# Three more projection chunks as seven products of quarter blocks, and the last block's sixteen selection rounds in one run

## The reference, cut to what matters

```
h = rmsnorm(x) ; z = h @ w_in          # 10 column groups
qa, ka, va (512 each), qi (4x64), ki (64), wi (4), qb, kb, vb, gb (512 each)
rope on qa, ka, qi, ki, qb, kb
indexer scores: sum over 4 heads of wi * relu(qi . ki), causal
per token: top 128 keys by that score (top 64 for a sample token)
a = softmax attention of 8 heads over the chosen keys only
b = retention of 8 heads with decay, group norm, gate
x = x + rmsnorm([a, b] @ w_out)
x = x + rmsnorm(relu(rmsnorm(x) @ w_up)^2 @ w_down)
```

## Time and profile before

| | us |
|---|---|
| median of 3 runs | 1571.54 (1571.03 to 1572.36) |
| the profiled execution's own time | 1573.14 |
| its span | 1571.4 |
| TensorE busy | 1547.7 (98%) |
| VectorE busy | 845.1 (54%) |
| ScalarE busy | 450.0 (29%) |
| GpSimd busy | 476.1 (30%) |

### The profile page before, as it was taken

How to read it: one execution, slowest core, us unless ns; L and a number is a source line. 1 busy time by engine, 2 the same in 40 slices (tenths; PEclk the granted TensorE clock), 3 DMA queues, 4 the chain that set the end, 5 groups by cost and what they waited for, 6 DMA issues and landing times.

```text
span 1571.4 us, 21618 instructions
## 1 busy us (share of the span) xinstructions
PE 1547.7 (98%) x7966; PEld 1154.9 (73%) x7966; DVE 845.1 (54%) x1708; ACT 450.0 (29%) x1045; POOL 476.1 (30%) x354
## 2 busy tenths in 40 slices
PE   8999999999999999999999999999999999999998
PEld 5445755688888888888844466556888888888887
DVE  4599679846652013333467977788366610132334
ACT  5222355225421003310242224551253200123101
POOL 0005201023653424345310051010146524234461
PEclk9999999999999999999999999999999999999999
DMA  6326311024332122222223272110243421322211
GB/s 211 131 72 215 135 55 54 3 86 133 131 112 88 74 108 81 86 73 84 94 72 108 81 235 89 54 55 14 74 147 122 135 80 54 112 103 81 80 55 55
DMA packets 52811, 150.40 MB, mean 96 GB/s; under 512 B 8250, under 2 KB 29506, under 8 KB 39394
## 3 DMA queue, kind: packets, MB, share of 16 engines
q1 hardware_dynamic: 45218, 140.65, 26.1%
q10 hardware_dynamic: 7488, 8.36, 1.5%
HBM read 139.79 MB, written 9.02 MB: 95 GB/s over the span
## 4 chain that ended last, share of the span: by engine, by line
PE 77%; DVE 18%; issue 2%; ACT 2%; POOL 0%; DMA 0%; ACTq 0%; DVEq 0%; POOLq 0%
PE ps L1186 46%; PE ps L806 9%; PE ps L1124 7%; PE ps L843 4%; DVE arena L1870 3%; DVE top L1868 3%; PE ps L771 1%; DVE x_feat L2024 1%; PE ps L784 1%; DVE arena L1814 1%; DVE arena L1816 1%; PE ps L971 1%; DVE rstd_ffn L1812 1%; PE ps L1082 1%; PE ps L994 1%
## 5 line engine op out<-in xcount | busy, mean ns | idle before, releaser
L806 PE MATMUL ps<-wring,h_feat 128*128 128x512 f32 (+1 forms) x704 | 316.3, 586 | 2.8 <-ACT h_feat L1309 2.5
L1186 PE MATMUL ps<-arena,wring 128*128 128x256 f32 (+1 forms) x1280 | 285.8, 382 | 0.3 <-DVE arena L2108 0.3
L1186 PEld LDWEIGHTS ps<-arena,wring 128*128 128x128 f32 x1280 | 243.0, 190 | 37.7 <-DVE arena L2108 1.1
L806 PEld LDWEIGHTS ps<-wring,h_feat 128*128 128x128 f32 x704 | 124.7, 190 | 125.7 <-issue 112.5
L2405 POOL TENSOR_TENSOR wring<-wring,arena 128x512 f32<-128x512 f32 (+1 forms) x48 | 78.8, 1641 | 345.3 <-PE ps L1186 321.9
L1186 PE MATMUL ps<-h_feat,wring 128*128 128x256 f32 (+1 forms) x768 | 176.6, 381 | 0.0
L1186 PEld LDWEIGHTS ps<-h_feat,wring 128*128 128x128 f32 x768 | 145.9, 190 | 21.6
L1186 PE MATMUL ps<-mix,wring 128*128 128x256 f32 (+1 forms) x512 | 120.2, 383 | 0.8 <-DVE p_sb L2082 0.8
L1186 PE MATMUL ps<-arena 128*128 128x264 f32 x512 | 119.1, 386 | 0.0
L1124 PE MATMUL ps<-mix,wring 128*128 128x256 f32 (+1 forms) x512 | 115.1, 384 | 0.8 <-ACT mix L1473 0.8
L2388 POOL TENSOR_TENSOR pt_sb<-pt_sb 128x256 f32<-128x256 f32 (+1 forms) x94 | 72.8, 774 | 126.4 <-ACT pt_sb L1283 123.1
(11 more groups left out here) (251 smaller groups left out, 2041.8 us busy)
## 6 DMA issues: line engine op xcount, KB each, us to landing
wring<-in_w_all SPq DMA_DIRECT2D x108, 1024.0 KB, 5.1
arena<-in_cache_k SPq DMA_DIRECT2D x32, 256.0 KB, 5.2
arena<-in_cache_v SPq DMA_DIRECT2D x32, 256.0 KB, 4.4
o_k_out<-arena ACTq DMA_DIRECT2D x2, 1024.0 KB
o_v_out<-arena ACTq DMA_DIRECT2D x2, 1024.0 KB
arena<-in_state SPq DMA_DIRECT2D x2, 1024.0 KB, 4.8
o_rets_out<-arena ACTq DMA_DIRECT2D x2, 1024.0 KB, 9.8
wring<-in_w_idx SPq DMA_DIRECT2D x3, 648.0 KB, 4.9
```

The lines of the kernel that those rows point to most:

```text
L806: last = mm(ps[:, bank_of(c, i), 0:width], h_feat[:, k, token_cols(t)], wt, start=(k == 0), stop=(k == KD - 1))
L1186: last = mm(out, a[:, j, :], b, start=(opens(n) and j == 0), stop=(j == nk - 1), skip_group_check=True)
```

## The change

`BLOCKED` becomes (1, 2, 3, 4, 5): chunks 1, 2 and 3 are done as seven products too. VectorE gets their five sums each, GpSimd their four weight sums each, ScalarE takes and scales quarters in place of whole tiles. The input's sums are made right at the layer's start; since in1's first place is needed for the indexer keys of the cache and the gate, it first lies in `mix`, and a fifth `input_sum` makes it again in its old place for chunk 5. The weight sums of chunk 1 lie in `qT`. The work beside the chunks gets new positions, the new keys of the samples (`new_key`) come after GpSimd's first sums of chunk 3, the value outputs are issued later, and `own_values(1)` one part earlier. The order on VectorE is written anew: block 1's rounds are spread over chunks 1 to 3, block 2's lie beside chunks 3 and 4, and block 3's sixteen rounds stand in one run after `chunk_c22(4)`, ahead of attention.

```diff
-BLOCKED = (4, 5)
+BLOCKED = (1, 2, 3, 4, 5)
...
+DOTS = [(3, 2), (4, 0), (4, 6), (5, 4), (6, 2), (7, 0)]
...
         def tokens_of(c):
-            return zr[1] if c == 4 else zr[0]
+            return {1: zr[1], 2: zr[0], 3: v_tok, 4: zr[1], 5: zr[0]}[c]
...
             def beside_q(i, k):
-                if (i, k) == (0, KD - 1):
+                if (i, k) == (2, 3):
...
                     pe.wait_ge(rope_done, past(rope_done) + TILES)
...
             def beside_qb(i, k):
...
-                if (i, k) in ((3, KD - 1), (6, 5)):
-                    g = (i - 3) // 3
+                if (i, k) in ((2, 3), (5, 3)):
+                    g = (i - 2) // 3
...
-                project(1, beside_q)
-                project(2, beside_k)
-                project(3, beside_v)
+                project_blocks(1, beside_q)
+                project_blocks(2, beside_k)
+                project_blocks(3, beside_v)
...
 VectorE, the layer's loop:
+                rope(1, NT)
+                for j in range(4):
+                    combine(j)
+                chunk_u2(1)
+                combine(4)
+                combine(5)
+                select_top(sc[1], top8[:], 1)
+                combine(6)
+                combine(7)
+                chunk_u3(1)
+                chunk_c22(1)
+                combine(8)
+                combine(9)
+                select_top(sc[1], top8[:], 1)
+                combine(10)
+                combine(11)
+                chunk_c12(1)
+                rope(1, 2)
+                rope(1, 3)
+                chunk_c21(1)
+                select_top(sc[1], top8[:], 1)
                 rope(1, 0)
...
+                rope(1, 1)
                 dve.wait_ge(ts_mm, past(ts_mm) + 1)
+                rope(2, NT)
...
+                select_top(works[:], tops[:], 4)
+                chunk_u2(2)
+                select_top(works[:], tops[:], TOPK_S // 8 - 4)
...
+                chunk_u3(2)
+                chunk_c22(2)
+                select_top(sc[1], top8[:], 2)
+                chunk_c12(2)
                 rope(2, 2)
                 rope(2, 3)
+                chunk_c21(2)
+                select_top(sc[1], top8[:], 1)
+                rope(2, 0)
+                rope(2, 1)
+                select_top(sc[1], top8[:], TOPK_P // 8 - 7)
+                block_mask(1)
+                chunk_u2(3)
+                select_top(sc[2], top8[:], 2)
+                chunk_u3(3)
+                chunk_c22(3)
...
-                select_top(sc[3], top8[:], 4)
+                chunk_c21(3)
+                select_top(sc[2], top8[:], 9)
                 chunk_u2(4)
-                select_top(sc[3], top8[:], TOPK_P // 8 - 15)
-                block_mask(3)
+                select_top(sc[2], top8[:], TOPK_P // 8 - 13)
+                block_mask(2)
                 own_values(0)
                 chunk_u3(4)
                 chunk_c22(4)
+                select_top(sc[3], top8[:], TOPK_P // 8)
+                block_mask(3)
...
 GpSimd, the layer's loop:
                 input_sum(1)
                 input_sum(2)
                 input_sum(3)
-                chunk_sum(4, 1)
-                chunk_sum(4, 2)
+                chunk_sum(1, 1)
+                chunk_sum(1, 2)
                 input_sum(4)
-                chunk_sum(4, 3)
-                chunk_sum(4, 4)
+                chunk_sum(1, 3)
+                chunk_sum(1, 4)
                 for n in range(1, 5):
-                    chunk_sum(5, n)
+                    chunk_sum(2, n)
+                chunk_sum(3, 1)
+                chunk_sum(3, 2)
+                for b in range(CSLOTS):
+                    new_key(b)
+                chunk_sum(3, 3)
+                for b in range(CSLOTS, NB):
+                    new_key(b)
+                chunk_sum(3, 4)
+                input_sum(5)
+                for c in (4, 5):
+                    for n in range(1, 5):
+                        chunk_sum(c, n)
```

More of the change, by code:

```diff
@@ L354, in quarter @@
             return a[:, at:at + 4 * 2 * P].rearrange("p (k n) -> p k n", n=2 * P)
-        in1, in2, in3, in4 = quarter(gate_flat, 3 * W), quarter(mix_high, 0), quarter(mix_high, 2 * W), quarter(temps, 0)
-        cs1, cs2 = quarter(kbd_flat, 0), quarter(kbd_flat, 2 * W)
+        in1, last_in1 = quarter(mix_flat, 0), quarter(gate_flat, 3 * W)
+        in2, in3, in4 = quarter(mix_high, 0), quarter(mix_high, 2 * W), quarter(temps, 0)
+        first_cs, cs = [[quarter(a, 2 * i * W) for i in range(2)] for a in (qT.rearrange("p h n -> p (h n)"), kbd_flat)]
         raw = [temps[:, i * W:(i + 1) * W] for i in range(3)]
@@ L578, in tokens_of, with sums_of_chunk, first_sum_of @@
         def tokens_of(c):
-            return zr[1] if c == 4 else zr[0]
+            return {1: zr[1], 2: zr[0], 3: v_tok, 4: zr[1], 5: zr[0]}[c]
+        def sums_of_chunk(c):
+            return first_cs if c == BLOCKED[0] else cs
+        def first_sum_of(c):
+            return last_in1 if c == BLOCKED[-1] else in1
         def quad_of(c, which):
@@ L825, in project_blocks @@
                         pe.wait_ge(in_sums, past(in_sums) + 2)
+                    if n == 5 and c == BLOCKED[-1]:
+                        pe.wait_ge(in_sums, past(in_sums) + 5)
                     if n == 7:
@@ L1575, in _ @@
                 act.wait_ge(ts_read, up(ts_read))
+                take_groups([qT[:, 3, :]])
+                scale_quad(2, "22", proj_c22)
+                scale_quad(2, "12", proj_c12)
+                take_p1(3)
+                scale_quad(2, "21", proj_c21)
+                evacuate(3, 1)
+                take_first(3)
+                take_groups([kT[:, h, :] for h in range(2)])
+                take_p5(3)
+                take_groups([kT[:, h, :] for h in range(2, 4)])
                 act.dma_start(k_out[bass.ds(l, 1)].rearrange("a (t p) n -> p (a t) n", p=P), zr[0][:, 0:NT, :]).then_inc(out_k, 16)
                 act.dma_start(ks_out[bass.ds(l, 1)].rearrange("a p n -> (a p) n"), zr[0][0:NB, NT, :]).then_inc(out_k, 16)
-                evacuate(3, 2)
-                evacuate(3, 3)
-                evacuate(3, 4)
                 for g in range(2):
```

171 lines of the change are left out of this document (88 added, 83 removed).

## The result

The changed kernel takes 1625.11 us, the median of four runs (1624.27 to 1626.54); the kernel before took 1571.95 beside it. The ratio is 1.0337, 95% interval 1.0319 to 1.0355. Predicted were 1622 us and a range of 1592 to 1634. The profiled execution has a span of 1622.4 us, 51.0 more than before. Two executions, one of experiment 11's kernel (4629.78 us) and one of the kernel before beside it (2011.41 us), ran at a granted TensorE clock of 0.33 and 0.75 throughout, and the ratios leave them out.

A forecast was written before the change was run, and what follows sets the result against it. TensorE, busy 98%, was the bound by the page, but would wait for VectorE before attention's step 2. Net joint 22.0, GpSimd meetings 26.6 and slow clock 2.0 made 50.6 us on 1573.1: 1623.7, so 1622 us, range 1592 to 1634.

The forecast's parts named there:

- TensorE's saving: Chunks 1 to 3 as seven products: 3.8 us a chunk, 11.3 us for three, 22.7 us in two layers.
- The joint: Attention's step 2 waits for VectorE's 27.0 us after product 7 of chunk 4; TensorE idles 21.3 us in the first layer.
- The wait by order: Chunk 2's sample tile waits 2.5 us for the bank of chunk 1's product 4, which VectorE reads late.
- (a): Chunk 0's rotations meet GpSimd's sums; the first transposes wait 4.4 us in layer 1, 5.9 in layer 2.
- (b): GpSimd's sums 1 and 2 of chunk 2 meet the last two indexer sums: 3.6 us, 3.3 reaching TensorE.
- (c): GpSimd's sums 3 and 4 of chunk 2 meet two rotations; product 7 of chunk 2 gets its bank 3.2 us late.
- (d): Chunk 3's sums 3 and 4 and the last input sum meet a rotation: 3.3 us at product 7, 1.6 taken.
- TensorE after a stop: Half pace after the 21 us stop at attention's step 2: 1.0 us a layer taken, bounds 0 and 3.0.
- The run alone: Rival, 20%: ports and clock cost nothing, VectorE's meetings falling into waits it has anyway; 1593.5 us.
- The cover that holds: Rival, 3%: TensorE work between product 7 of chunk 4 and step 2 hides VectorE; the 22.7 us gain arrives, 1549.
- The case worse than the sum: Rival, 12%: full 3.3 us at product 7 of chunk 3, token factors, 3 us a layer of slow TensorE; 1633.
- Products that don't get cheaper: Rival, 3%: switching operands eats the 3.8 us a chunk, 22.7 us more, 1645.

The follow-up runs named there:

- experiment 11: Kernel before, with GpSimd's input and weight sums in four pieces each and nothing else: 1572.38 us, ratio 0.9994.
- Experiment 1: Kernel before, with block 3's sixteen rounds and mask in one run after `chunk_c22(4)`: 1609.88 us, ratio 1.0248.
- experiment 2: Changed kernel with block 3's sixteen rounds left out, its mask still made: 1578.12 us, ratio to the kernel before 1.0033.
- Experiment 4: Changed kernel, with the second layer's GpSimd weight sums of chunks 1 to 3 made for 16 of 256 columns only: 1611.43 us, ratio 1.0258.
- experiment 6: Changed kernel, with 23 extra matmuls into an unused bank ahead of the wait of attention's step 2: 1624.89 us.
- experiment 3: Changed kernel, with block 3's sixteen rounds spread, five before attention and eleven inside it: 1603.18 us, ratio 1.0199.
- experiment 8: Kernel before, with chunk 3 alone added as seven products and VectorE and GpSimd work reordered around it: 1589.99 us, ratio 1.0118.
- experiment 9: Kernel of experiment 8, with GpSimd's input and weight sums in four pieces of 128x256: 1572.36 us, ratio 1.0006 to the kernel before.

## Why the prediction was right

**TensorE's saving (right).** From chunk 1's start to the end of product 7 of chunk 4 the trace has 141.9 us. Less the waits (13.2) and the slow clock at the transposes (2.4), that leaves 126.3. The forecast was the 135.4 of before less 11.3, and 1.9 more for the moved values: 126.0. But the 135.4 hold 1.2 us of waits (0.41, 0.61 and 0.22), which the forecast left in; without them it would be 124.8, so about 1.5 us of the 11.3 did not come. Where they went is open.

**The joint (right).** VectorE's 27.0 us from the end of product 7 to step 2 were 27.14, and the stop of 21.3 was 21.18 in the first layer and 21.17 in the second. Experiment 1 shows the run as a cause by itself (38.8 us), experiment 2 that removing it returns 47.0 of the 53.2.

**The wait by order, and the meetings (right in place, a little high in size).** Forecast and trace, in us of TensorE's wait:

| | forecast | measured |
|---|---|---|
| (a) first transposes, layer 1, layer 2 | 4.4, 5.9 | 4.32, 5.28 |
| order and (b), chunk 2's first product and sample tile | 2.5 + 3.3 | 2.65 + 2.56 |
| (c) product 7 of chunk 2 | 3.2 | 2.73 |
| (d) product 7 of chunk 3 | 1.6 | 0.97 |

Experiment 4 shows GpSimd's sums as the cause of all but 1.2 and 1.9 us of these waits, in the layer where they were thin. The prediction says that the rounds were the only thing beside GpSimd's sums in the kernel before; its own row at 146.67 shows a scaling there, so what the rows supported was that the rounds keep their time and other instructions may not. Why two waits around the sample tile share the sum otherwise than I wrote was not tried.

**TensorE after a stop (the term that was mis-sized).** The forecast had 1.0 a layer, at the joint alone. There it was 0.7 net (experiment 6): 2.6 us on the rows, the rest hidden behind VectorE as the prediction had argued. What it missed is the same fall behind the 4.3 us stop at the transposes, where nothing hides it: twelve transposes and half a product take 5.96 us (2.90 and 3.06) where they took 3.6 before, 2.4 us more, and 2.1 in the second layer. So the term was 6 us and not 2. The prediction held that no row shows a stop within the kernel doing this, but the earlier trace rows have one: behind the 1.17 us wait at 924.69 ten records take 3.85 us, where ten took 2.42 in the first layer (at 146.28), and the granted clock was half:

```profile
926.00:928.60 2.60, 2.60 (x8) 1.96 (x8) 2.46 (x7) 1.36 (x4) 0.05 (x1) 0.50 0.98 401
```

The prediction booked these 1.4 us as lost time and did not ask what had slowed the row. The waits, 27.4 us of 31.5 forecast in the two layers, made up for it by chance, and the forecast came closer than its terms. On the profiled executions the forecast of 1623.7 stands against 1624.3; the other 2.5 us between 1622 and 1625.1 are how these two executions lie to their medians. TensorE's busy time fell by 12.9 us and not by 20, because its rows at half clock are some 10 us longer.

The Trainium skill (TensorE: Matmul & The Clock Gate, "Part 1: The HAM clock gate (the "warmup" mystery)") says that the engine drops to half its clock after an idle stretch. The rows agree at 4.3 and 21 us of stop, and at 1.17 us in the kernel before. At 2.65 us they show both: clock kept in the changed kernel, lost in experiments 2 and 3.

**Rivals.** The run alone (1593.5) fell with the waits at (a) to (c). The cover that holds (1549) had its point of decision right, 27 us of work, and nothing near it was there (6.0 us). The case worse than the sum (1633) had the slow clock right, 3.1 and 2.8 us in the two layers for its 3, and product 7 of chunk 3 wrong, 0.97 us for its 3.3. Products that don't get cheaper fell with 3.46 us a product in all chunks.

## What to carry to other kernels

A share of busy time of half says nothing on room: VectorE at 54% had no place for 24 us in one piece ahead of a wait, nor for 17 us in the steps behind it. When work is moved between engines, walk the queue of the engine that gets it up to the next point at which the bound engine needs its result. Where GpSimd and VectorE work side by side on SBUF, cut GpSimd's instructions short, or lay them beside selection rounds (MAX8, MATCH_REPLACE8), which kept their times: the same sums in one piece each cost 17.6 us more than in four (experiments 8 and 9). One tensor input is no safe sign; a TENSOR_SCALAR with one took 1.58 us for 0.36. A gain on the bound engine also has to be matched by every chain that was just in time before, DMAs included; move those first.

## What the hardware showed that I had not expected

- A stop of 4.3 us in the middle of a busy stretch halves TensorE's clock for some 5 us (0.50 in the window from 39.5 to 42.7, 1.00 from 45.6). One of 2.65 us did it in two kernels and not in another, and one of 1.17 us did it in the kernel before.
- A slow clock behind a stop costs next to nothing when the engine that caused the stop is still late: 19.91 us of extra matmuls in the stop changed the time by no more than can be told (0.2 us).
- Four GpSimd instructions of 128x256 took 2.8 us against 2.4 for one of 128x1024, and that price did not show in any time (experiment 11).
